# A hybrid decoder step on one core: token groups of 256 and 304 columns instead of 304 and 256, with the expert work laid out for them

## What is computed

```
p = rmsnorm(h) @ w_in                       # 8 heads x (q,k,v,z of GDN; q,k,v,gate of FoX)
o_gdn = gated delta rule, exact, in chunks  # state S passed from chunk to chunk
o_fox = softmax(q k^T + decay) v            # causal; samples also over 256 cached rows
h = h + concat(norm(o_gdn)*silu(z), norm(o_fox)*sigmoid(og)) @ w_out
x = rmsnorm(h); scores = (x @ w_query) . sub_keys   # 8 heads, top 16 of 128x128 experts
y = h + sum over heads, k of  gate * gelu(x . expert_u[idx]) * expert_v[idx]
```

## Time and profile before

| | |
|---|---|
| median of 3 runs | 4961.61 us (4955.26 to 4962.0) |
| the profiled execution | 4960.07 us, its span 4958.2 us |
| instructions | 35078 |
| busy, share of the span | PE 49%, VectorE 68%, POOL 48%, ScalarE 11% |
| mean DMA rate | 299 GB/s |

### The profile page before, as it was taken

How to read it: one execution, slowest core, us unless ns; L and a number is a source line. 1 busy time by engine, 2 the same in 40 slices (tenths; PEclk the granted TensorE clock), 3 DMA queues, 4 the chain that set the end, 5 groups by cost and what they waited for, 6 DMA issues and landing times. The chain is left out here.

```text
span 4958.2 us, 35078 instructions
## 1 busy us (share of the span) xinstructions
PE 2435.6 (49%) x11665; PEld 1945.6 (39%) x11665; DVE 3370.0 (68%) x4430; ACT 541.9 (11%) x1360; POOL 2376.5 (48%) x1230
## 2 busy tenths in 40 slices
PE   5999999979783877777764535310000000000000
PEld 4777777766663766666653434210000000000000
DVE  1233333330287588988886558988779998889888
ACT  1222222220001122222220000000000000000000
POOL 1000000000002366666656534447778887878886
PEclk8999999989896999888885767655555555555555
DMA  5655555513334799999998888878999999999998
GB/s 153 187 167 167 163 167 163 159 58 122 108 93 181 290 404 403 403 406 396 397 349 333 340 303 302 318 271 367 380 359 417 421 416 407 406 394 422 401 397 356
DMA packets 486235, 1480.39 MB, mean 299 GB/s; under 512 B 41180, under 2 KB 324624, under 8 KB 326520
## 3 DMA queue, kind: packets, MB, share of 16 engines
q0 software_dynamic: 162208, 1158.46, 58.2%
q1 hardware_dynamic: 314632, 252.58, 16.7%
q10 hardware_dynamic: 9216, 67.11, 3.3%
HBM read 1384.56 MB, written 93.32 MB: 298 GB/s over the span
## 5 line engine op out<-in xcount | busy, mean ns | idle before, releaser
L1778 DVE CUSTOM_DVE_ANT_0 ex_ring<-ex_ring,ex_xi 128x2048 f32<-128x2048 f32 x544 | 1244.3, 2289 | 160.2 <-DMA ex_ring<-in_peer_u_dram,idx_all 69.2
L1791 DVE SCALAR_TENSOR_TENSOR ex_y<-ex_ring,ex_wt,ex_y 128x2048 f32<-128x2048 f32 x539 | 1266.5, 2350 | 108.9 <-DMA ex_ring<-in_peer_v_dram,idx_all 81.6
L1729 POOL DMA_INDIRECT ex_ring<-in_peer_u_dram,idx_all x384 | 801.1, 2086 | 329.9 <-issue 109.3
L1729 POOL DMA_INDIRECT ex_ring<-in_peer_v_dram,idx_all x384 | 829.5, 2160 | 234.6 <-DVE ex_hid L1778 128.2
L785 PE MATMUL heads_a_pj<-xnT_a,heads_a_w 128*128 128x304 f32 x2048 | 622.1, 441 | 19.3 <-DMA heads_a_w<-in_w_in_dram 19.3
L785 PE MATMUL heads_b_pj<-xnT_b,heads_b_w 128*128 128x256 f32 x2048 | 548.7, 413 | 17.9 <-DVE mixT_b L1456 9.5
L1729 POOL DMA_INDIRECT ex_ring<-in_peer_v_dram,ex_idx_s x160 | 328.8, 2055 | 281.8 <-DVE ex_hid L1778 239.7
L785 PEld LDWEIGHTS heads_b_pj<-xnT_b,heads_b_w 128*128 128x128 f32 x2048 | 408.4, 211 | 73.9 <-DVE mixT_b L1456 12.6
L785 PEld LDWEIGHTS heads_a_pj<-xnT_a,heads_a_w 128*128 128x128 f32 x2048 | 380.4, 199 | 133.5 <-issue 23.0
L1729 POOL DMA_INDIRECT ex_ring<-in_peer_u_dram,ex_idx_s x160 | 300.2, 1877 | 208.8 <-DVE ex_y L1791 149.1
L1581 POOL TENSOR_TENSOR heads_a_ub<-heads_a_uN,const 128x1024 f32<-128x1024 f32 x8 | 15.2, 1896 | 559.0 <-ACT heads_a_uN L1176 559.0
(11 more groups left out here) (552 smaller groups left out, 3537.7 us busy)
## 6 DMA issues: line engine op xcount, KB each, us to landing
heads_a_w<-in_w_in_dram SPq DMA_DIRECT2D x64, 1024.0 KB, 6.0
w_scratch<-heads_a_w ACTq DMA_DIRECT2D x64, 1024.0 KB, 4.2
heads_b_w<-w_scratch SPq DMA_DIRECT2D x64, 1024.0 KB, 9.1
out_a_w<-in_w_out_dram SPq DMA_DIRECT2D x8, 2048.0 KB, 9.0
route_a_w<-in_peer_w_query_dram SPq DMA_DIRECT2D x16, 1024.0 KB, 5.9
out_b_w<-in_w_out_dram SPq DMA_DIRECT2D x8, 2048.0 KB, 29.8
route_b_w<-in_peer_w_query_dram SPq DMA_DIRECT2D x16, 1024.0 KB, 8.6
heads_a_kc<-in_cache_k_dram SPq DMA_DIRECT2D x128, 64.0 KB, 2.9
```

The source lines that it names most:

```text
L1729: pool.indirect_dma_start(self.ring[:, i % RING, :], None, self.tables[which], bass.IndirectOffsetOnAxis(ap=self.index(s, g, k), axis=0)). ...
L1778: nc.vector.tensor_tensor_reduce(ring, ring, self.xi[:], 1.0, 0.0, ALU.mult, ALU.add, self.hid[:, g % 2, k:k + 1]).then_inc(self.sem["cons ...
L1791: nc.vector.scalar_tensor_tensor(y, ring, wt, y, ALU.mult, ALU.add).then_inc(self.sem["consumed"], 1)
```

## The change

The groups change places: FIRST gets 256 columns in two tiles of 128, LATER 304 in tiles of 128, 128 and 48. What is one tile less in the first five stages is one tile more in the next five. The constants are split, since some are used by FIRST alone (`const_first`), and `heads` of LATER keeps three weight buffers instead of four.

The expert sets are laid out again. FIRST keeps 128 tokens of its second tile as a whole set (8 groups); 64 prompt tokens of its first tile become a set of two halves with four heads each (4 groups); the samples are a set as before (2 groups). The other 16 prompt tokens of that tile are joined with the 48 of LATER's last tile to another set of two halves (4 groups), run with LATER. Groups and items stay 34 and 1,088, but FIRST now has 14 groups (448 items) where it had 18 (576), and the item order is in two runs: the first 14 groups end with v items alone before the run of the other 20 begins with u items alone. The stages of LATER carry all 448 (14, 330, 48, 8, 48), and `gather` may not run ahead of item 448 until `rest_of_experts`. That phase has 640 items instead of 604, and fills the table of the new joined set at its start.

```diff
-FIRST = Group("a", 0, (0, 112, 240, 304), 0)
-LATER = Group("b", 304, (0, 128, 256), 3)
+FIRST = Group("a", 0, (0, 128, 256), 0)
+LATER = Group("b", 256, (0, 128, 256, 304), 2)
...
-OVERLAP = {"norm": 12, "heads": 320, "out": 48, "ffn": 8, "route": 96}
+OVERLAP = {"norm": 14, "heads": 330, "out": 48, "ffn": 8, "route": 48}
...
-    W, PJ = (5, 3) if samples else (4, 2)
+    W, PJ = (5, 3) if samples else (3, 2)
...
-    pj, R1, R2, F = [buf[f"pj{i}"] for i in range(PJ)], B.R1, B.R2, (B.F2, B.F1)
+    pj, R1, R2, F = [buf[f"pj{i}"] for i in range(PJ)], B.R1, B.R2, (B.F2, B.F1) if samples else (B.F1, B.F2)
...
+        def split(r, group, tile, rows):
+
+            first = group.base + group.tiles[tile][0] - T0
+            p = r * half + (P - T0 - half if group is LATER else 0)
+            return self.Part(p, group, tile, rows, r * HEADS // 2, y_prompt[first + rows.start:first + rows.stop])
         fold = P // NS
         self.sets, places = [], 0
         for group, parts, groups in (
             (FIRST, [prompt_part(0, FIRST, 1)], HEADS),
-            (FIRST, [prompt_part(0, FIRST, 0), prompt_part(half, FIRST, 2)], HEADS),
+            (FIRST, [split(r, FIRST, 0, slice(T0, T0 + half)) for r in range(2)], HEADS // 2),
             (FIRST, [self.Part(r * NS, FIRST, 0, slice(0, NS), r * HEADS // fold, y_sample) for r in range(fold)], HEADS // fold),
             (LATER, [prompt_part(0, LATER, 0)], HEADS),
+            (LATER, [split(r, *p) for r in range(2) for p in ((FIRST, 0, slice(T0 + half, P)), (LATER, 2, slice(0, LATER.rows[2])))],
+             HEADS // 2),
             (LATER, [prompt_part(0, LATER, 1)], HEADS),
...
+        self.cut = max(s.end for s in self.sets if s.group is FIRST)
+        self.known = 2 * TOPK * self.cut
...
+    def run(self, g):
+
+        return (0, self.cut) if g < self.cut else (self.cut, self.groups - self.cut)
...
-        for i in range(self.issued, min(taken + RING, self.items)):
+        for i in range(self.issued, min(taken + RING, self.known)):
...
-            if r > 0 and part.slot == s.parts[r - 1].slot:
+            if any(part.slot == other.slot for other in s.parts[:r]):
                 pool.wait_ge(self.sem["y_out"], 16 * self.y_outs)
...
 def rest_of_experts(nc, stream):
     with ExitStack() as ctx:
         block = ctx.enter_context(nc.Block())
+        stream.known = stream.items
+
+        @block.sync
+        def _(sp):
+            stream.spread(sp, LATER)
```

More of the change, by code:

```diff
@@ L110, in constant_parts @@
         "after": np.concatenate(after, 1),
[L111 to L112 removed]
+        "not_upto": np.concatenate([np.where(m, 0.0, NEG) for m in upto], 1),
+        "not_after": np.concatenate([np.where(m, 0.0, NEG) for m in after], 1),
         "levels": np.concatenate(levels[:1] + [m.T for m in levels[1:]], 1),
@@ L125, in constant_parts @@
         "row": row,
+        "valid": row < LATER.rows[-1],
+        "causal_mixed": np.where((row >= NS) & (first_keys > row - NS), NEG, 0.0),
+        "causal0": np.where(same0 & (col <= row) | (row >= NS), 0.0, NEG)[:, :NS],
+        "batch_cols": np.broadcast_to((np.arange(NS)[None, :] // NQ == np.arange(NB)[:, None]).reshape(1, -1),
+                                      (P, NB * NS)),
     }
@@ L202, in build @@
         with ExitStack() as first:
+            keep(first, "const_first", [P, width - lasting])
             keep(first, "logf_past", [P, PAGES, HEADS])
@@ L333, in _ @@
             if stream:
-                stream.spread(sp)
+                stream.spread(sp, FIRST)
+            else:
+                sp.wait_ge(sem["first_in"], 16)
             sp.wait_ge(sem["logf_ready"], 1)
@@ L601, in heads @@
     gap = P - group.rows[0]
+    whole = N // P
     SEGMENTS = 8 * HEADS
@@ L759, in fox @@
                             sp.wait_ge(sem[f"f_{own}_copied"], n)
-                            sp.dma_start(out[group.seq:KW, h, :].rearrange("(t p) d -> p t d", p=P), rows[:]
+                            end = group.seq + whole * P
+                            sp.dma_start(out[group.seq:end, h, :].rearrange("(t p) d -> p t d", p=P), rows[:, 0:whole, :]
                                          ).then_inc(sem[f"{own}_kept"], 16)
+                            sp.dma_start(out[end:KW, h, :], rows[0:KW - end, whole, :]).then_inc(sem[f"{own}_kept"], 16)
             Marks(gdn(), fox(), weights(), *([cached()] if samples else [])).run()
@@ L1192, in stored @@
                 if h > 0 and (own == "v" or not samples):
-                    act.wait_ge(sem[f"{own}_kept"], (16 * T if samples else 16) * h)
+                    act.wait_ge(sem[f"{own}_kept"], 32 * h)
             def fox():
@@ L1696, in gates, with spread @@
         return self.gate_s[:, at:at + TOPK]
-    def spread(self, sp):
+    def spread(self, sp, group):
         for s in self.sets:
-            for part in s.parts if not s.whole else []:
+            for part in s.parts if not s.whole and s.group is group else []:
                 for table, source in ((self.idx_s, self.mem["idx_all"]), (self.gate_s, self.mem["gate_all"])):
@@ L1705, in spread, with spread_all @@
                                  ).then_inc(self.sem["spread"], 16)
-    def spread_all(self):
-        return sum(32 * len(s.parts) for s in self.sets if not s.whole)
+    def spread_all(self, group):
+        return sum(32 * len(s.parts) for s in self.sets if not s.whole and (s.group is FIRST or s.group is group))
     def gather(self, pool, taken):
-        for i in range(self.issued, min(taken + RING, self.items)):
+        for i in range(self.issued, min(taken + RING, self.known)):
             which, g, k = self.item(i)
@@ L1769, in take @@
             which, g, k = self.item(i)
-            s, ring, turn = self.set_of[g], self.ring[:, i % RING, :], g + 2 * which
-            if i == self.turn_first(turn) and turn >= 2:
-                self.weigh(dve, turn - 2)
+            s, ring = self.set_of[g], self.ring[:, i % RING, :]
+            first, groups = self.run(g)
+            if which == 0 and k == 0 and g - first >= 2:
+                self.weigh(dve, g - 2)
+            elif which == 1 and k == 0 and g - first >= groups - 2:
+                self.weigh(dve, g)
             if which == 0:
```

69 lines of the change are left out of this document (35 added, 34 removed).

## The result

The changed kernel takes 4796.02 us, the median of 4 runs (4781.12 to 4801.85), against 4959.82 us of the kernel before (4 runs): a ratio of 0.9666, 95% interval 0.9642 to 0.969. The forecast was 4858 us in a range of 4795 to 4940, so the time lies at the lower end of the range. Its direction and its first part hold; the second part gets longer by 119 us where 190 were said. The profiled execution took 4798.93 us (span 4797.2), 161.1 us less than that of before; the forecast was 102 us less.

A forecast was written before the change was run, and what follows sets the result against it. TensorE (VectorE in routing) was taken to bound the first 1552 us, mostly DMA and the items the rest; -292 us in FIRST, +93 in LATER's stages and +97 in the last phase gave -102: 4858 us, range 4795 to 4940.

The forecast's parts named there:

- first part: FIRST's five stages, before any item runs: less TensorE and VectorE work makes them 292 us shorter.
- second part: From LATER's stages to the end: LATER's stages get 93 us longer and the last phase 97 us.
- LATER's heads: LATER's heads stage: ten more items and the third tile's work add 70 us, twice the DMA's own.
- (b): LATER's heads become a chain of VectorE and TensorE, +130 us instead of +70: 4918 us; chance 0.15.
- (e): LATER's heads take TensorE's added work whole at a lower clock, +189 us instead of +70: 4977 us, slower; chance 0.06.
- (c): FIRST's heads are held by a head's chain, not TensorE's work, and give only 87 us: 4934 us; chance 0.06.
- (d): Matmul spacing hardly follows the columns; FIRST's projections give 33 us instead of 90: 4915 us; chance 0.03.
- the last phase: Final phase after LATER's stages: 36 more items, and fixed costs from 112 to 120 us, make it 97 us longer.
- out_b: LATER's out stage: more matmuls per step, period half the sum of weight landing and step, +28 us.
- LATER's routing: LATER's routing stage: 48 fewer items for VectorE, plus 20 us for the half sets' sums, net -32 us.
- ffn_b: LATER's ffn stage: one more tile adds 12 us.
- (a): LATER's heads stay on DMA alone, +34 us, and LATER's out stage hides its new matmuls: 4794 us; chance 0.10.

The follow-up runs named there:

- b_table: The kernel before with only its table of item shares replaced by the changed kernel's (14, 330, 48, 8, 48): 4982.34 us, ratio 1.0037.
- b_out_more: The kernel before with tile 0 multiplied a second time in each step of LATER's out stage, result thrown away: 4952.5 us, ratio 0.9987.
- a_r96: The changed kernel with 48 items moved from LATER's heads to its routing (282 and 96 instead of 330 and 48): 4792.05 us, ratio 0.965.

## Why the prediction was right and where it was not

**The first part** was said to give 292 us and gave 279.6. Its steps hold one by one (norm, out, ffn and routing within 5 us each). FIRST's heads gave 149.3 us where 163 were forecast; TensorE was busy 840.6 us for 823. In runs of the same stage at a granted clock of 0.94 it was busy 814 to 815 us and the stage took 841 to 843 us, 18 us less than forecast. So the count of work was right to 9 us, and the rest is the clock.

**LATER's heads**, +63.6 us for +70, are right in the main reason: most of 173 us of TensorE work is hidden under the items. The two parts are less good than their sum. The ten items cost 37.5 us (b_table) where 26 were charged, and the third tile 26 us where 44 were (8 for the wider first projections, and 36 that were a guess, "twice the DMA's own"). The misses have opposite signs, so a part of the agreement is luck. TensorE is busy 927 us where 957 were counted, VectorE 974 us as counted. Rivals (b) and (e) fall with it, (c) by FIRST's heads, and (d) by the spacing of 226 ns.

**The step that failed** is the pricing of LATER's small stages and of the last phase, where each addition was put on the path at nearly its full size. Four terms were mis-sized, 67 us together.
- out_b, +28 us forecast, +7.8 measured. The period as half the sum of step and landing took the landing of 29.8 us as a constant; it was that of two loads on the way at once. With the steps longer, the added 57 us of TensorE work cost nothing (-11 us in the stage in b_out_more, -12 in a_r96). What the stage did get longer by is a change of sets of some 19 us, which the forecast did not have in it.
- LATER's routing, -32 forecast, -48.9 measured. The items' part was right (111 us counted, 113 in b_table). The 20 us for chained sums of the half sets show as one wait of 8.3 us, and VectorE is busy 275.7 us where 285 were counted.
- ffn_b, +12 forecast, +0.2 measured; without items the third tile costs 5.9 us there.
- the last phase, +97 forecast, +79.4 measured. 36 items were right (89 counted, +87.6 in b_table); the fixed part was said to go from 112 to 120 us and fell. Some 9 of the 18 us are in the stops of over 5 us, which were to grow by 8 us and went from 77.4 to 76.5: the landing was added to the barrier wait of 15.6 us whose place it takes, while the samples' chain was put 6 us too low and the joined set's sums 6 too high. The other 9 are not in any single stop and were not parted.

LATER's heads add 6 us to these 67; the 12 us that the first part gave less and norm_b's 1.5 count against them. That is the 59 us between 102 and 161. Rival (a), 4794 us, comes out at the time measured, with out_b hidden as it said, but its heads on DMA alone did not happen: it has the right time by luck, from the terms of the other stages.

## What to carry to other kernels

It pays to move work from a stretch where its engine sets the time to one where another resource mostly does. Here 312 us of stage time taken from FIRST came back as 307 in LATER when nothing ran beside it; under the gathers 280 us were taken and came back as 112. The gain is the cover, not the count of work. Two kernels without the covering work, run beside the two with it, tell this apart at once.

A transfer's landing is priced only with the transfers that were on their way beside it: the same 2 MB loads took 29.8 us in the median when two were on the way under the gathers, 23.4 when they were asked for further apart, and 8.6 without gathers. And where a stop is removed and another put in its place, subtract the one before adding the other.

The length of a stop is not what its removal gives. 32.6 us of waits for sums removed gave 14.4 us or, against the other profile of the changed kernel, 10.4; 31.1 us of stops with an empty ring gave 14.8. Profiles of the changed kernel's last phase differ by 4 us among themselves (1699.0 and 1695.0), so these shares are rough.
